# Keeping x with its channels on partitions through a fp32 decoder trunk

## The reference, cut to what matters

```python
D_MODEL, SEQ, DEPTH, D_FF, MEM_LEN = 1024, 256, 2, 2816, 256     # float32, batch 1

def rms_norm(x, g):
    return x * lax.rsqrt(jnp.mean(x * x, axis=-1, keepdims=True) + EPS) * g

def swiglu(h, w_gate, w_up, w_down):
    return (jax.nn.silu(h @ w_gate) * (h @ w_up)) @ w_down

for l in range(DEPTH):
    x = x + 0.5 * swiglu(rms_norm(x, ffn1_norm[l]), ...)            # stage ffn1
    z = rms_norm(x, mix_norm[l]) @ w_in[l]                          # stage in
    ...                                                             # attention, two convolutions
    x = x + jnp.concatenate([o_att, o_cc, o_sc], axis=-1) @ w_out[l]  # stage out
    hq = rms_norm(x, xa_norm[l]) @ xa_wq[l]                         # stage q
    kv = rms_norm(mem, mem_norm[l]) @ xa_wkv[l]                     # stage kv
    ...
    x = x + o @ xa_wo[l]                                            # stage o
    x = x + 0.5 * swiglu(rms_norm(x, ffn2_norm[l]), ...)            # stage ffn2
return rms_norm(x, final_norm)
```

## Time and profile before

| | us |
|---|---|
| median of three runs | 1140.85 |
| the profiled execution | 1141.1 |
| its span, first to last instruction | 1139.3 |
| TensorE busy | 1131.4 (99%) |
| weight loads of TensorE busy | 976.9 (86%) |
| VectorE busy | 857.4 (75%) |
| ScalarE busy | 647.1 (57%) |
| GpSimd busy | 21.8 (2%) |
| bytes read | 208.85 MB, 184 GB/s over the span |

### The profile page before, as it was taken

The page is one execution under the profiler, slowest core; times in us unless marked ns, Lnnn a source line. Parts: engine busy times, 40 slices in busy tenths (PEclk is TensorE's granted clock), DMA queues, the critical chain, the costliest instruction groups (busy, mean ns, idle before and its releaser), DMA issues.

```text
span 1139.3 us, 15680 instructions
## 1 busy us (share of the span) xinstructions
PE 1131.4 (99%) x6180; PEld 976.9 (86%) x6180; DVE 857.4 (75%) x1164; ACT 647.1 (57%) x937; POOL 21.8 (2%) x63
## 2 busy tenths in 40 slices
PE   9999999999999999999999999999999999999997
PEld 8888888888889888888888888888888898888886
DVE  7877676899967686766777676669998676866765
ACT  6555556547755554544565555464577556645454
POOL 1000000000000000000000000000000000000000
PEclk9999999999999999999999999999999999999999
DMA  7966654644444366555547655544545444666561
GB/s 265 327 202 188 218 186 147 221 149 165 170 159 172 111 224 217 164 201 199 186 151 255 219 161 205 192 165 168 186 148 204 166 146 125 210 190 216 183 200 43
DMA packets 66266, 210.92 MB, mean 185 GB/s; under 512 B 5009, under 2 KB 24209, under 8 KB 61073
## 3 DMA queue, kind: packets, MB, share of 16 engines
q1 hardware_dynamic: 65216, 209.26, 54.0%
q10 hardware_dynamic: 976, 0.66, 0.2%
HBM read 208.85 MB, written 1.05 MB: 184 GB/s over the span
## 4 chain that ended last, share of the span: by engine, by line
PE 94%; DVE 4%; DVEq 1%; ACT 0%; issue 0%
PE G L1720 28%; PE G L1729 14%; PE D L1567 10%; PE D L1565 10%; PE D L1566 10%; PE G L1660 3%; PE G L1565 3%; PE G L1567 3%; PE G L1566 3%; PE D L1660 2%; DVE w_lo L1006 2%; PE G L1669 1%; DVE acc L1215 1%; PE D L1669 1%; PE D L1632 1%; DVEq L1217 1%
## 5 line engine op out<-in xcount | busy, mean ns | idle before, releaser
L1006 DVE TENSOR_TENSOR w_lo<-w_raw,w_hi 128x2048 fp32r<-128x2048 f32 (+3 forms) x260 | 452.6, 1746 | 54.8 <-ACT w_hi L595 54.0
L595 ACT ACTIVATE w_hi<-w_raw 128x2048 fp32r<-128x2048 f32 (+3 forms) x260 | 381.1, 1475 | 35.2 <-PE D L1567 17.0
L1720 PE MATMUL G<-a,w_hi 128*128 128x512 f32 x1406 | 346.3, 391 | 0.1
L1720 PEld LDWEIGHTS G<-a,w_hi 128*128 128x128 f32 x1406 | 256.1, 188 | 48.6 <-issue 1.1
L1729 PEld LDWEIGHTS G<-a,w_lo 128*128 128x128 f32 x1406 | 175.4, 188 | 8.6
L1729 PE MATMUL G<-a,w_lo 128*128 128x256 f32 x1406 | 177.5, 277 | 0.0
L1111 DVE TENSOR_TENSOR zqk<-G,zqk 128x512 f32<-128x512 f32 x88 | 60.8, 691 | 127.3 <-ACT zqk L674 123.3
L1565 PE MATMUL D<-w_hi,hT_hi 128*128 128x512 f32 x352 | 137.2, 390 | 0.0
L1567 PE MATMUL D<-w_hi,hT_lo 128*128 128x512 f32 x352 | 137.0, 389 | 0.0
L1566 PE MATMUL D<-w_lo,hT_hi 128*128 128x512 f32 x352 | 136.9, 389 | 0.0
L674 ACT ACTIVATE zqk<-G 128x512 f32<-128x512 f32 x88 | 52.2, 593 | 143.1 <-PE G L1729 143.1
(11 more groups left out here) (261 smaller groups left out, 1282.5 us busy)
## 6 DMA issues: line engine op xcount, KB each, us to landing
w_raw<-w_dram SPq DMA_DIRECT2D x120, 1024.0 KB, 5.0
w_raw<-w_dram SPq DMA_DIRECT2D x143, 512.0 KB, 5.3
m_raw<-memT_dram SPq DMA_DIRECT2D x2, 1024.0 KB, 8.8
w_raw<-w_dram SPq DMA_DIRECT2D x6, 256.0 KB, 6.5
w_raw<-w_dram SPq DMA_DIRECT2D x8, 128.0 KB, 3.8
vx<-mem_dram SPq DMA_DIRECT2D x1, 1024.0 KB, 10.8
x<-x_dram SPq DMA_DIRECT2D x2, 256.0 KB, 5.7
gbc<-fin_dram SPq DMA_DIRECT2D x1, 512.0 KB, 6.6
```

Of the source, the lines that this page charges most:

```text
L595: A(w_hi[:, part(i)], w_raw[:, part(i)], ACT.Copy).then_inc(s_hi, 1)
L1006: V.tensor_tensor(w_lo[:, part_lo(i)], w_raw[:, part(i)], w_hi[:, part(i)].bitcast(F32), ALU.subtract).then_inc(s_lo, 1)
L1720: last = M(banks[b], whi[:, at:at + P], both, start=k == 0 and not low_first, stop=k == KD - 1 and low_first, skip_group_check=low_first)
```

## The change

x lies with channels on partitions, as 8 blocks of 128 channels by 256 tokens, from the first norm to the last stage. The parts:

- down, out and o make 256-column products with the weights stationary and the activations moving, three for each block of 128 by 128 weights; their result is already laid out as x. Gate and up make three products of 256 columns into the same half bank, in place of one of 512 and one of 256.
- The transposes at the start of the seven later stages go. The first x is transposed as before, and ScalarE copies it out of PSUM (`copy_first_x`) before the first down block.
- The mean square is a sum over partitions: ScalarE squares x, VectorE adds the 8 blocks (`channel_squares`), and TensorE multiplies the sum by a column of ones (`mean_squares`, two plain fp32 products of one column), ahead of the last quarter of the stage's first blocks; ScalarE copies the two columns for GpSimd.
- `copy_tail` and `pair_sum` go; `pair_scale` reads PSUM. A chunk takes one bank of four, and waits for the scaling of the chunk four before it.
- `b` (a second view of the room of `a`) and the hidden tiles start 16 elements past the other tiles; `w_lo` of the FFN blocks has no shift any more.
- In the last stage (q = 7) the results must have tokens on partitions: 2x is transposed into the banks by 16 plain fp32 products (`residual_by_token`), down runs with activations stationary in products of 256 columns, and the sums of the last norm are read from PSUM.

```diff
 def lo_is_stationary(name):
     stage, piece = name[1], name[2]
-    if stage in ("ffn1", "ffn2"):
-        return piece[0] == "gu"
     return stage == "q" or (stage == "kv" and piece < 4) or (stage == "in" and piece in (7, 8))
...
-        x = sb("x", [P, TT, D])
-        a = sb("a", [P, KD, 2, T], F32R)
+        x = sb("x", [P, KD, T])
+        a_room = sb("a", [P, 2 * KD * T + OFF], F32R)
...
+        a, a_hi, a_lo = activations(0)
+        b, b_hi, b_lo = activations(OFF)
+        hT_hi = sb("hT_hi", [P, SLOTS_H, T], F32R)
+        hT_lo = sb("hT_lo", [P, SLOTS_H, T], F32R)
+        sb("line_m", [P, OFF])
...
             def norm_start(q):
-                squares(q, 0)
-                a_hi_part(q, range(4))
-                squares(q, 1)
-                a_hi_part(q, range(4, 8))
+                def high(j):
+                    act.wait_ge(s_xup, 4 * (q - 1) + j + 1)
+                    for k in (2 * j, 2 * j + 1):
+                        A(to[:, k, :], x[:, k, :], ACT.Copy, scale=gain(NORMS[q % 4], k)).then_inc(s_ahi, 1)
+                def squares(j):
+                    A(squared[j // 2][:, j % 2, :], x[:, 2 * j:2 * j + 2, :].rearrange("p k t -> p (k t)"), ACT.Square,
+                      scale=D ** -0.5).then_inc(s_sq, 1)
+
+                high(0)
+                high(1)
+                squares(0)
+                high(2)
+                squares(1)
+                high(3)
+                squares(2)
+                squares(3)
...
+            def mean_squares(q):
+                act.wait_ge(s_stat, q)
+                A(mean_sq[:, :], STAT_BANKS[q % 4][:, 0:TT], ACT.Copy).then_inc(s_ssq, 1)
+            def copy_first_x():
+                for j in range(4):
+                    A(x[:, j::4, :], pair(DB[j]), ACT.Copy).then_inc(s_xcopy, 1)
...
-            def copy_tail(l, f, c):
-                act.wait_ge(s_blk, gu_end(l, f, c))
-                A(tail[:, :, :], GG[:, 2 * (c % 2):2 * (c % 2) + 2, T:], ACT.Copy).then_inc(s_tail, 1)
...
             def norm_lo(q):
-                a_lo_part(q, range(0, 2))
-                second_half(q - 1)
-                a_lo_part(q, range(2, 8))
+                x_update(q - 1, 1)
+                for k in range(0, 2):
+                    low_part(q, k)
+                x_update(q - 1, 2)
+                for k in range(2, 4):
+                    low_part(q, k)
+                x_update(q - 1, 3)
+                for k in range(4, 8):
+                    low_part(q, k)
+            def channel_squares(q):
+                dve.wait_ge(s_sq, 4 * q)
+                V.tensor_tensor(v_sb[:, :, :], v_sb[:, :, :], gbc[:, :, :], ALU.add)
+                dve.drain()
+                V.tensor_tensor(v_sb[:, 1, :], v_sb[:, 0, :], v_sb[:, 1, :], ALU.add)
+                dve.drain()
+                V.tensor_tensor(channel_sum, v_sb[:, 1, 0:T], v_sb[:, 1, T:], ALU.add).then_inc(s_chsum, 1)
...
-            def pair_sum(l, f, c):
-                dve.wait_ge(s_tail, chunk(l, f, c))
-                V.tensor_tensor(gu[:, :, :], GG[:, 2 * (c % 2):2 * (c % 2) + 2, 0:T], tail[:, :, :], ALU.add
-                                ).then_inc(s_sum, 1)
...
+            def channel_products(d, hi, lo, whi, wlo, n, k, start, stop):
+                w = slice(n * D + d * P, n * D + (d + 1) * P)
+                M(channels(d), whi[:, w], hi[:, k, :], start=start and d % 2 == 0, stop=False, skip_group_check=True)
+                M(channels(d), whi[:, w], lo[:, k, :], start=False, stop=False, skip_group_check=True)
+                return M(channels(d), wlo[:, w], hi[:, k, :], start=False, stop=stop, skip_group_check=True)
...
             def last_down(q, hi, lo, ks):
-                for c in range(2):
+                for d in range(KD):
                     for n, k in enumerate(ks):
...
-                            if (c, n, t) == (1, 1, 1):
-                                pe.wait_ge(s_xup, 4 * q + 2)
-                                x_transposes(q + 1, range(4))
-                    if c == 0:
-                        last.then_inc(s_half, 1)
+                        last = channel_products(d, hi, lo, whi, wlo, n, k, False, n == 1)
+                    if d in (1, 3, 5):
+                        last.then_inc(s_bank, 1)
...
+            def residual_by_token():
+                for k in range(KD):
+                    for t in range(TT):
+                        M(DB[2 * (k // 4) + t][:, k % 4 * P:(k % 4 + 1) * P], x[:, k, tok(t)], twice,
+                          start=k % 4 == 0, stop=False, skip_group_check=True)
...
+            def mean_squares(q):
+                pe.wait_ge(s_chsum, q)
+                for t in range(TT):
+                    last = M(STAT_BANKS[q % 4][:, t:t + 1], channel_sum[:, tok(t)], ones[:, 0:1], start=t == 0, stop=True,
+                             skip_group_check=True)
+                last.then_inc(s_stat, 1)
...
             def gate_up(l, f, c, ks, ready=None):
+                for k in ks:
+                    if ready is not None:
+                        pe.wait_ge(s_alo, ready + k + 1)
+                    for u in range(2):
+                        out = G[c % 4][:, u * T:(u + 1) * T]
+                        w = slice((2 * (k - k0) + u) * P, (2 * (k - k0) + u + 1) * P)
+                        M(out, whi[:, w], b_hi[:, k, :], start=(k, u) == (0, 0), stop=False, skip_group_check=True)
+                        M(out, whi[:, w], b_lo[:, k, :], start=False, stop=False, skip_group_check=True)
+                        last = M(out, wlo[:, w], b_hi[:, k, :], start=False, stop=k == KD - 1, skip_group_check=True)
```

More of the change, by code:

```diff
@@ L30 @@
 SLOTS_H = 4
+OFF = 16
 OUT_ORDER = (3, 2, 0, 1)
@@ L1601, in down @@
                         between()
-                    for c in range(2):
-                        w = slice(n * D + c * N, n * D + (c + 1) * N)
-                        for t in range(TT):
-                            last = product(DB[2 * c + t][:, :], hi[:, k, tok(t)], lo[:, k, tok(t)], whi[:, w],
-                                           wlo[:, w], start and n == 0, False)
+                    for d in range(KD):
+                        last = channel_products(d, hi, lo, whi, wlo, n, k, start and n == 0, False)
                 last.then_inc(s_blk, 1)
@@ L1956, in out @@
                     k = 2 * A_PAIR[i]
-                    down(l, "out", i, a_hi, a_lo, (k, k + 1), False, between=between)
+                    down(l, "out", i, b_hi, b_lo, (k, k + 1), False, between=between)
                 def columns_free():
```

421 lines of the change are left out of this document (200 added, 221 removed).

## The result

The changed kernel took 1157.68 us (median of 6 runs, 1150.80 to 1158.18) beside 1140.76 us before on the same chip: ratio 1.013, 95% interval 1.0112 to 1.0148. It is slower by 1.3%, where 1134.2 us was forecast. Four of its runs lie within 1157.7 and 1158.2 and two at 1150.8 and 1150.9; the experiments show what such a pair of levels is in a kernel close to this one. The profiled execution took 1157.68.

A forecast was written before the change was run, and what follows sets the result against it. TensorE was taken to bound the kernel, without gaps. Terms -12.3 + 3.4 + 3.3 + 0.3 - 0.6 = -5.9, with -0.7 for heads -6.6, gave 1134.2 us from 1140.85; own range 1129 to 1139, stated range 1128 to 1148.

The forecast's parts named there:

- the price of a product of 256 columns: Gate-up, down, out and o: 7104 products replacing others taken at 113.7 ns, 0 us; ends 113.0 (-5 us) and 114.5 (+6 us).
- rows 4 and 5: Unbroken 256-column streams before the change: stage in block 6 at 119.8 ns, stage q at 117.5 ns a product.
- the cheap row: Gate-up run of 30 low-weight products before the change, weights 16 elements past the moving tile: 113.7 ns each.
- the 115.8 ns of the heads: Stage heads, alternating product forms: 115.8 ns a unit; one form alone might return half the excess, -0.7 us at seven heads.
- Loads meet the stream: Rival: weight loads meet moving reads in gate-up and down, 117.5 to 119.8 ns a product, +27 to +43 us; chance 0.18.
- The mark set for it: Two chunks with two downs should take 16.4 us from start to start; 17 us means the loads collide.
- Mean squares: Sum over channels on TensorE: four records and a late next product, 0.49 us each, seven times +3.4 us.
- the late norm: Rival: the norm's engine chain comes 1 us late at each of seven seams, 7 us come back, 1141; chance 0.07.
- Residual: Last stage, residual by token: 16 plain products, 32 records, +3.3 us (3.1 to 3.6).
- Seams: Stage starts needing low parts of x in time: 0 to 1 us at the three tightest, +0.3 us in all.
- Transposes: Seven later stages lose 16 transposes each: 14 groups of 0.88 us go, -12.3 us on TensorE.
- The end: Closing pass: without VectorE's addition ScalarE squares sooner, but scales the other half first; -0.6 us (-0.9 to 0).

## Why the prediction was wrong

**The step that failed** is the price of a product of 256 columns: 113.7 ns taken, 117.16 found as the mean over the 7104, so 3.46 x 7.1 = +24.6 us in place of 0. I had two dear rows of unbroken streams and a cheap one that stood between products of 512 columns, and took the cheap one as nearest "in distance, form and neighbours". In neighbours it was the farthest: a chunk of the kernel after is all products of 256 columns, as rows 4 and 5 are. The kernel before with its halves shows the cheap row turning dear with its products unchanged. The rows that I had written down held the warning as well: the eight low-weight products from 578.03 to 578.97 have the same 16 elements between and took 117.5 ns each. In the trace of the kernel before, 39 runs of 30 such products stand at 113.5 ns, but eight of the 14 runs of eight stand at 117.8. I put the 115.8 ns of the heads down to the alternation of forms and didn't see in it a second price of the same product. The ends of the term, 113.0 to 114.5, left the trace's own 117.5 out, and the chance of 0.18 for the rival was too low.

**The rival that came true** is "Loads meet the stream", with its place and its mechanism as far as the distance matters (0 to 64 elements move the time from 1142.5 to 1178.2). Its band, 117.5 to 119.8 ns or 1161 to 1178 us, was a touch high: the measured 1157.68 lies 3 us below it, since a seventh of the products stayed at 113.3 ns and the other terms brought 1.4 us more than their sum. It was in the prediction as a fixed price of a place; the runs show at least two prices for one place, at 16 and at 48 elements. The mark set for it, 16.4 us for two chunks and 17 at a collision, read 16.96.

**The other terms held together.** Their sum was -6.6 us and came out 0.9 to 1.6 lower. The forecast of the profiled execution with the measured price in place of 113.7:

| kernel | mean ns of the 7104 | 1134.5 + 7.10 x (mean - 113.7) | measured |
|---|---|---|---|
| after | 117.16 | 1159.1 | 1157.68 |
| 0 elements | 119.98 | 1179.1 | 1178.18 |
| 48, first execution | 114.11 | 1137.4 | 1136.47 |
| 48, second | 115.03 | 1143.9 | 1142.28 |

Four executions with 42 us between them are met within 0.9 to 1.6 us, always from above. What is left is in these rows of the kernel after. TensorE at the seam from stage o, at `mean_squares` and at the residual by token:

```profile
391.39 0.31 PE L1769 MATMUL G<-a,w_hi 128*128 128x256 f32 x1
391.54 0.28 PE L1770 MATMUL G<-a,w_hi 128*128 128x256 f32 x1
...
399.90 0.50 PE L1692 MATMUL D<-ones,v_sb 128*128 128x1 f32 x4
400.26 0.36 PE L1769 MATMUL G<-a,w_hi 128*128 128x256 f32 x1
400.46 0.28 PE L1770 MATMUL G<-a,w_hi 128*128 128x256 f32 x1
...
980.48 3.73 PE L1676 MATMUL D<-std,x 128*128 128x128 f32 x32
983.97 0.36 PE L1769 MATMUL G<-a,w_hi 128*128 128x256 f32 x1
984.18 0.28 PE L1770 MATMUL G<-a,w_hi 128*128 128x256 f32 x1
```

- Mean squares: 0.36 us for four records and 0.08 behind them, 0.44 against the 0.49 foreseen; no idle ahead of them, so the late norm didn't come.
- Residual: 3.49 and 0.09, 3.6 us against 3.3.
- Seams: where a stage begins with products of 256 columns, the largest step is 0.15 us (391.39 to 391.54), at two of the seven seams; where it begins with products of 512, the first steps are 0.22 to 0.24. 0.3 in all was foreseen. The 0.2 to 1.4 us of room were enough.
- Transposes: the 14 groups are gone, and no group stands in their place.
- The end: from the last start of a product, 1150.43, to the end of the span at 1155.9 are 5.5 us, against 1139.3 - 1132.69 = 6.6 before: -1.1 where -0.6 was foreseen. That is half a microsecond of the remainder. How the rest splits between the heads and the transposes wasn't taken apart.

So the change does gain 7.5 to 8.2 us by its other parts (the 6.6 of the sum and this remainder), and gives 24.6 back by the price of its products. With 48 elements it gives back 3 to 9 us.

## What to carry to other kernels

The price of a short product belongs to the stream it stands in, not to its shape: take it from a row where the same kind stands alone for dozens in a line, and when the only such rows are the dear ones, they are the forecast. Where one product shows two prices in one trace, as here in the earlier trace rows, the dearer one is a term of its own. Before halves replace wholes on a bound engine, the halves alone are worth a run in the old kernel; here that one edit shows 22 us. Where streams of short products with a weight load each can't be avoided, the start of the moving tile is worth a sweep: nine distances lay 36 us apart, with no order by which a tenth could be told, and the change with 48 elements in place of 16 (1142.5 us, 1136.3 to 1143.1) is as fast as the kernel before, though not shown faster.

## What the runs showed of the hardware

- A stream of products of 256 columns, each with its own load of weights, has distinct paces: 113.3 ns (most of the stream at 48 elements, a seventh at 16), 117.8 (the rest at 16), 118.8 (32), 119.9 to 120.0 (0, 24 and 64), and means of 117.3, 118.1 and 118.2 at 8, 40 and 56, at a granted clock of 0.999 to 1.0 throughout.
- At 48 elements the pace is turned over by the down by token followed by gate-up (9 of 9 in each of two executions) and by the two products with `mean_r` (12 of 12); at 16 by gate-up followed by the down by token (10 of 10, but none of 11 behind a chunk that began with a product of 512 columns).
- A pace holds over a whole stage, across changes of bank, ring place and tile, and can differ between two executions of one program: 113.3 or 117.8 ns in the first FFN stage, 5.8 us of the time. The two levels of the kernel after, 6.9 us apart, are as much as 1584 products of one stage at 4.4 ns; it wasn't profiled at the lower one, so there this is worked out and not shown.
- Not settled: by what mechanism a pause or a crossing turns the pace over, why it is another crossing at 16 than at 48 elements, whether a single product would also bring the fast pace back, and why 24 elements are as dear as 0 while 48 are cheap.
